# Mixture of experts on one core: gathering the tokens of eight experts at once, 40 places each, with two more weight slots

## The reference, cut to what matters

```python
g_sel = argmax(xt @ w_rg + b_rg)                 # one group per token
top_v, top_i = top_k(el_sel, 2)                  # two experts in it
gate = softmax(top_v) * p_sel                    # their weights
hid = silu(xb @ w_gate[e]) * (xb @ w_up[e])      # for the tokens xb of expert e
y[token] += (hid @ w_down[e]) * gate
ys = (silu(xt @ ws_gate) * (xt @ ws_up)) @ ws_down
y = y + sigmoid(xt @ w_sg) * ys
```

## Time and profile before

| | before |
|---|---|
| median of 3 runs | 2825.86 us (2825.48 to 2827.86) |
| profiled execution, its own time | 2827.91 us |
| its span, first to last instruction | 2826.1 us |
| mean granted TensorE clock | 0.976 |
| PE busy | 2671.8 us (95%) |
| DVE, ACT, POOL busy | 1230.1, 1096.6, 83.3 us |
| HBM read | 697.21 MB, 247 GB/s over the span |

### The profile page before, as it was taken

The page is one execution under the profiler, slowest core; times in us unless marked ns, Lnnn a source line. Parts: engine busy times, 40 slices in busy tenths (PEclk is TensorE's granted clock), DMA queues, the critical chain, the costliest instruction groups (busy, mean ns, idle before and its releaser), DMA issues.

```text
span 2826.1 us, 48229 instructions
## 1 busy us (share of the span) xinstructions
PE 2671.8 (95%) x20460; PEld 2084.1 (74%) x20460; DVE 1230.1 (44%) x2087; ACT 1096.6 (39%) x1999; POOL 83.3 (3%) x100
## 2 busy tenths in 40 slices
PE   8999888999998999999899999999898999999998
PEld 6879756887887887788787666666698776666665
DVE  5547257655556744655562112122476432112112
ACT  5445244545445623644542222222463532222222
POOL 0000000000000011000010000000002100000000
PEclk9999889999999999999999999999999999999999
DMA  8534574644544421454354999999641149999996
GB/s 341 188 123 166 211 308 197 247 185 160 213 179 164 150 77 62 158 215 179 120 200 189 411 413 417 416 412 417 264 152 61 46 169 394 415 417 413 416 417 247
DMA packets 96419, 701.53 MB, mean 248 GB/s; under 512 B 10688, under 2 KB 10816, under 8 KB 11328
## 3 DMA queue, kind: packets, MB, share of 16 engines
q1 hardware_dynamic: 96192, 698.30, 62.3%
HBM read 697.21 MB, written 1.05 MB: 247 GB/s over the span
## 4 chain that ended last, share of the span: by engine, by line
PE 88%; DVE 5%; ACT 3%; issue 2%; DMA 1%; POOL 0%; SPq 0%; DVEq 0%; ACTq 0%
PE bank L1597 16%; PE bank L834 12%; PE bank L836 12%; PE bank L835 12%; PE bank L1657 8%; PE bank L1575 5%; PE bank L1684 4%; PE bank L1930 3%; DMA weight_ring<-weight_slots 1%; PE bank L2050 1%; PE bank L1466 1%; PE bank L1469 1%; PE bank L1481 1%; PE bank L1090 1%; PE bank L561 1%
## 5 line engine op out<-in xcount | busy, mean ns | idle before, releaser
L1597 PE MATMUL bank<-weight_ring,packed_h 128*64 128x256 f32 x2176 | 285.4, 379 | 0.0
L834 PE MATMUL bank<-source_hi_lo,weight_hi_lo 128*128 128x256 f32 x864 | 250.9, 290 | 13.3 <-DVE source_hi_lo L824 8.9
L1597 PE MATMUL bank<-more_slots,packed_h 128*64 128x256 f32 x1920 | 257.0, 379 | 1.5 <-ACT packed_h L1584 1.5
L834 PE MATMUL bank<-gate_up_hi_lo,x_hi_lo 128*128 128x512 f32 x640 | 253.1, 396 | 0.5 <-DVE gate_up_hi_lo L952 0.5
L1597 PEld LDWEIGHTS bank<-weight_ring,packed_h 128*64 128x64 f32 x2176 | 196.3, 137 | 74.3 <-issue 18.1
L836 PE MATMUL bank<-gate_up_hi_lo,x_hi_lo 128*128 128x512 f32 x640 | 249.7, 390 | 0.0
L835 PE MATMUL bank<-gate_up_hi_lo,x_hi_lo 128*128 128x512 f32 x640 | 249.3, 389 | 0.0
L835 PE MATMUL bank<-source_hi_lo,weight_hi_lo 128*128 128x256 f32 x864 | 245.7, 284 | 0.0
L836 PE MATMUL bank<-source_hi_lo,weight_hi_lo 128*128 128x256 f32 x864 | 245.5, 284 | 0.0
L1597 PEld LDWEIGHTS bank<-more_slots,packed_h 128*64 128x64 f32 x1920 | 173.9, 137 | 69.8 <-issue 15.4
L793 DVE TENSOR_TENSOR weight_hi_lo<-weight_ring,weight_hi_lo 128x1024 fp32r<-128x1024 f32 x141 | 171.7, 1222 | 89.2 <-ACT weight_hi_lo L787 89.0
(11 more groups left out here) (590 smaller groups left out, 4982.1 us busy)
## 6 DMA issues: line engine op xcount, KB each, us to landing
weight_ring<-weight_slots SPq DMA_DIRECT2D x443, 1024.0 KB, 7.6
more_slots<-weight_slots SPq DMA_DIRECT2D x212, 1024.0 KB, 9.1
h_sb<-weight_slots SPq DMA_DIRECT2D x3, 1024.0 KB, 7.0
y_sb<-weight_slots SPq DMA_DIRECT2D x3, 1024.0 KB, 9.5
params_sb<-small_params SPq DMA_DIRECT2D x1, 2908.5 KB, 17.2
x_sb<-x_by_tokens SPq DMA_DIRECT2D x1, 1024.0 KB, 5.2
out_by_tokens<-x_sb SPq DMA_DIRECT2D x4, 256.0 KB, 2.5
params_sb<-small_params SPq DMA_DIRECT2D x1, 70.5 KB, 5.0
```

What stands on the lines that cost most here:

```text
L834: e.matmul(out, w[0], x[0], start=start, stop=False, skip_group_check=shared)
L1597: mm = e.matmul(ps[x * CAP:(x + 1) * CAP, m * FB:(m + 1) * FB], self.hc[:, c, (2 * (p % 2) + x) * CAP:(2 * (p % 2) + x + 1) * CAP], wt[:, ...
```

## The change

Places per expert go from 64 to 40, while the tiles of the expert products stay 64 wide (`TILE`). `select_dve` makes the matrix for eight experts at once, 320 columns, in every fourth pair; the gated copy stays a matter of four experts (`select_gates_dve`), in tiles of 64 of which 40 are written. `gather_pe` takes one chunk to a bank, four matmuls of 320 columns, eight times for eight experts; `gather_act` copies 320 columns at a time. Gathers stand in the pairs p = 3, 7, ... 27, four banks ahead of the scatter and four behind the transposes. The products of an expert read 64 columns of `hc` from its first place on, of which 24 are the next expert's. POOL clears the columns behind the last expert and the unused places of the gated copies at the start of the stage. The flag goes up above 40 tokens. The stage has seven slots of its own instead of five, `late_gates` and its transpose become parts of `packed_silu`, the unused constant goes, and the scratch size falls from 8192 to 1024.

```diff
...
 SLOT = 2048
 RING = 6
 FFN_EXTRA = 2
-MOE_EXTRA = 5
-CAP = 64
+MOE_EXTRA = 7
+CAP = 40
+TILE = 64
 FB = 256
 FFN_BLOCKS = 2816 // FB
 N_EXP = 64
...
-    pk.add("before", (s < t).astype(np.float32))
...
         self.picked, self.gates = sb("picked", [P, TT, N_EXP]), sb("gates", [P, TT, N_EXP])
         self.rank, self.most = sb("ranks", [P, TT, N_EXP]), sb("most_tokens", [P, 1])
         self.h_tok = sb("h_tokens_hi_lo", [P, 2, TT, D], F32R)
-        self.sel = [sb(f"places{j}", [P, TT, 4, CAP], F32R) for j in range(2)]
-        self.selg = [sb(f"gated_places{j}", [P, TT, 4, CAP]) for j in range(2)]
-        self.hc = sb("packed_h", [P, C, 4 * CAP])
-        self.late, self.gates_T = sb("late_gates", [P, N_EXP]), sb("late_gates_T", [N_EXP, T])
+        self.sel = [sb(f"places{j}", [P, TT, 8, CAP], F32R) for j in range(2)]
+        self.selg = [sb(f"gated_places{j}", [P, TT, 4, TILE]) for j in range(2)]
+        self.hc = sb("packed_h", [P, C, 7 * CAP + TILE])
         self.flag = k.flags[:, self.i:self.i + 1]
         inner = ExitStack()
...
         self.gate_sum, self.slot_gate = sb("gates_by_place", [P, T]), sb("place_gates", [P, 2])
         self.psilu = [sb(f"packed_silu{j}", [P, FB]) for j in range(2)]
         self.phid = [sb(f"packed_hidden{j}", [P, FB]) for j in range(2)]
+        self.late, self.gates_T = self.psilu[1][:, 0:N_EXP], self.psilu[0][0:N_EXP, :]
         self.shared_slots, waiting = [], []
...
         return buf[(p // 2) % 2][:, q, 2 * (p % 2):2 * (p % 2) + 2, :]
     def select_dve(self, e, g):
         k, n, b = self.k, self.n, g % 2
         if g == 0:
             e.wait_ge(*k.ge("ranks", n, TT - 1))
+        if g >= 2:
+            e.wait_ge(*k.ge("gathered", n, g - 2, C - 1))
+        for q in range(TT):
+            r = self.rank[:, q, 8 * g:8 * g + 8].unsqueeze(2).to_broadcast([P, 8, CAP])
+            e.tensor_tensor(self.sel[b][:, q, :, :], k.par("places").unsqueeze(1).to_broadcast([P, 8, CAP]), r, ALU.is_equal).then_inc(*k.up("places", n, g, q))
+    def select_gates_dve(self, e, h):
+        k, n, b, four_of = self.k, self.n, h % 2, slice(4 * (h % 2), 4 * (h % 2) + 4)
+        if h == 0:
             e.wait_ge(*k.ge("gates", n, TT - 1))
-        if g >= 2:
-            e.wait_ge(*k.ge("gathered", n, g - 2, 3))
-            e.wait_ge(*k.ge("turned_back", n, 2 * (g - 2) + 1))
+            e.wait_ge(*k.ge("empty_places", n, 2))
+        if h >= 2:
+            e.wait_ge(*k.ge("turned_back", n, 2 * (h - 2) + 1))
         for q in range(TT):
-            r = self.rank[:, q, 4 * g:4 * g + 4].unsqueeze(2).to_broadcast([P, 4, CAP])
-            e.tensor_tensor(self.sel[b][:, q, :, :], k.par("places").unsqueeze(1).to_broadcast([P, 4, CAP]), r, ALU.is_equal).then_inc(*k.up("places", n, g, q))
-            e.wait_ge(*k.ge("places", n, g, q))
-            e.tensor_tensor(self.selg[b][:, q, :, :], self.sel[b][:, q, :, :].bitcast(F32),
-                            self.gates[:, q, 4 * g:4 * g + 4].unsqueeze(2).to_broadcast([P, 4, CAP]), ALU.mult).then_inc(*k.up("gated_places", n, g, q))
-    def gather_pe(self, e, g, m):
-        k, n = self.k, self.n
-        ps = k.banks.take(e, (n, "gather", g, m), ("packed_h", n, g, m))
-        if m == 0:
+            e.wait_ge(*k.ge("places", n, h // 2, q))
+            e.tensor_tensor(self.selg[b][:, q, :, 0:CAP], self.sel[h // 2 % 2][:, q, four_of, :].bitcast(F32),
+                            self.gates[:, q, 4 * h:4 * h + 4].unsqueeze(2).to_broadcast([P, 4, CAP]), ALU.mult).then_inc(*k.up("gated_places", n, h, q))
+    def gather_pe(self, e, g, c):
+        k, n = self.k, self.n
+        ps = k.banks.take(e, (n, "gather", g, c), ("packed_h", n, g, c))
+        if c == 0:
             e.wait_ge(*k.ge("places", n, g, TT - 1))
-        if g == 0 and m == 0:
+        if g == 0 and c == 0:
             e.wait_ge(*k.ge("h_tok_lo", n, TT - 1, 1))
-        for j in range(2):
-            c = 2 * m + j
-            for x, (q, part) in enumerate((q, part) for q in range(TT) for part in range(2)):
-                mm = e.matmul(ps[:, j * T:(j + 1) * T], self.h_tok[:, part, q, c * P:(c + 1) * P],
-                              self.sel[g % 2][:, q, :, :].rearrange("p e s -> p (e s)"), start=x == 0, stop=x == 3)
-        mm.then_inc(*k.up("gathered", n, g, m))
-    def gather_act(self, e, g, m):
-        k, n = self.k, self.n
-        if g and m == 0:
-            e.wait_ge(*k.ge("packed_up", n, 2 * g - 1))
-        e.wait_ge(*k.ge("gathered", n, g, m))
-        e.activation(self.hc[:, 2 * m:2 * m + 2, :], halves(k.banks.at(n, "gather", g, m)), ACT.Copy).then_inc(*k.up("packed_h", n, g, m))
+        for x, (q, part) in enumerate((q, part) for q in range(TT) for part in range(2)):
+            mm = e.matmul(ps[:, 0:8 * CAP], self.h_tok[:, part, q, c * P:(c + 1) * P],
+                          self.sel[g % 2][:, q, :, :].rearrange("p e s -> p (e s)"), start=x == 0, stop=x == 3)
+        mm.then_inc(*k.up("gathered", n, g, c))
+    def gather_act(self, e, g, c):
+        k, n = self.k, self.n
+        if g and c == 0:
+            e.wait_ge(*k.ge("packed_up", n, 4 * g - 1))
+        e.wait_ge(*k.ge("gathered", n, g, c))
+        e.activation(self.hc[:, c, 0:8 * CAP], k.banks.at(n, "gather", g, c)[:, 0:8 * CAP], ACT.Copy).then_inc(*k.up("packed_h", n, g, c))
     def packed_gate_up_pe(self, e, p):
         k, n, w = self.k, self.n, self.expert_slots[p]
         ps = k.banks.take(e, (n, "packed", p), ("packed_hidden", n, p))
-        if p % 2 == 0:
-            e.wait_ge(*k.ge("packed_h", n, p // 2, 3))
+        if p % 4 == 0:
+            e.wait_ge(*k.ge("packed_h", n, p // 4, C - 1))
+        if p == 0:
+            e.wait_ge(*k.ge("empty_places", n, 0))
         for m in range(2):
             for c in range(C):
                 for x in range(2):
                     i, wt = w[2 * m + x]
                     if c == 0:
                         e.wait_ge(*k.weights.landed(i))
-                    mm = e.matmul(ps[x * CAP:(x + 1) * CAP, m * FB:(m + 1) * FB], self.hc[:, c, (2 * (p % 2) + x) * CAP:(2 * (p % 2) + x + 1) * CAP],
+                    first = (2 * (p % 4) + x) * CAP
+                    mm = e.matmul(ps[x * TILE:(x + 1) * TILE, m * FB:(m + 1) * FB], self.hc[:, c, first:first + TILE],
                                   wt[:, c * FB:(c + 1) * FB], start=c == 0, stop=c == C - 1)
             mm.then_inc(*k.up("packed_gate" if m == 0 else "packed_up", n, p))
...
                 i, wd = self.expert_slots[p][4 + x]
                 if fc == 0 and m == 0:
                     e.wait_ge(*k.weights.landed(i))
-                mm = e.matmul(ps[x * CAP:(x + 1) * CAP, :], self.turned[p % 2][:, fc * P + x * CAP:fc * P + (x + 1) * CAP],
+                mm = e.matmul(ps[x * TILE:(x + 1) * TILE, :], self.turned[p % 2][:, fc * P + x * TILE:fc * P + (x + 1) * TILE],
                               wd[:, fc * D + m * 512:fc * D + (m + 1) * 512], start=fc == 0, stop=fc == 1)
         mm.then_inc(*k.up("packed_down", n, p, m))
...
     def gathers_in(self, p):
-        g = p // 2 + 1
-        return (g, (0, 1), (2, 3)) if p % 2 and g < self.PAIRS // 2 else (g, (), ())
+        g = p // 4 + 1
+        return (g, (0, 1, 2, 3), (4, 5, 6, 7)) if p % 4 == 3 and g < self.PAIRS // 4 else (g, (), ())
     def experts_pe(self, e):
         for p in range(self.PAIRS):
...
         return over
     def experts_act(self, e):
-        for m in range(4):
-            self.gather_act(e, 0, m)
+        for c in range(C):
+            self.gather_act(e, 0, c)
         for p in range(self.PAIRS):
             if p == self.PAIRS - 1:
                 over = self.overflow_load(e)
...
             if p == self.PAIRS - 1:
                 over = self.overflow_load(e)
             self.packed_hidden_dve(e, p)
+            if p % 4 == 0 and p // 4 + 1 < self.PAIRS // 4:
+                self.select_dve(e, p // 4 + 1)
             if p % 2 == 0 and p // 2 + 1 < self.PAIRS // 2:
-                self.select_dve(e, p // 2 + 1)
+                self.select_gates_dve(e, p // 2 + 1)
             self.scatter_dve(e, p)
             self.packed_out_dve(e, p, 0)
             self.packed_out_dve(e, p, 1)
...
         self.shared_pe(e, 3)
         self.spread_pe(e, self.k.gain[:, self.i, 3, :])
         for m in range(4):
-            self.gather_pe(e, 0, m)
+            self.gather_pe(e, 0, 2 * m)
+            self.gather_pe(e, 0, 2 * m + 1)
             if m < 3:
                 self.shared_down_pe(e, m + 1)
         over = self.experts_pe(e)
...
             self.shared_dve(e, u)
         self.ranks_dve(e)
         self.select_dve(e, 0)
+        self.select_gates_dve(e, 0)
         self.shared_dve(e, 3)
         over = self.experts_dve(e)
         self.overflow_dve(e, over)
         self.back_dve(e, lambda f: k.ge("gain_row", self.n, f))
     def pool(self, e):
+        k, n = self.k, self.n
+        for signal in self.begun():
+            e.wait_ge(*k.ge(*signal))
```

(4 more changed lines are left out.)

## The result

| | before, same chip | changed |
|---|---|---|
| median of 4 runs | 2826.86 us (2825.48 to 2828.77) | 2795.90 us (2791.26 to 2799.56) |
| ratio | | 0.9893 (0.988 to 0.9905) |
| profiled execution | 2827.91 us | 2793.84 us, span 2792.0, mean granted clock 0.976 |
| params load | 2908.5 KB | 2832.5 KB |

The change makes the kernel 31 us faster, where 39.0 were forecast. The same file among the experiments gave 2792.26 us and 35 us. The first measurement lies 9 us above the forecast, outside the range that was given to the forecast's own mechanism (2782 to 2792) and at the upper edge of the wide one (2778 to 2796). The second lies 5 us above the forecast, at the edge of the narrow range.

A forecast was written before the change was run, and what follows sets the result against it. PE was taken to bound the mixtures, with weights close behind. Per stage -25.8 + 5.8 + 0.8 - 0.2 = -19.4 us; two stages -38.8, constant -0.2: -39.0, so 2786.9 us, range 2778 to 2796 (own 2782 to 2792).

The forecast's parts named there:

- the forecast's own mechanism: Whole kernel: PE stays the bound and the summed terms hold, 2786.9 us, own range 2782 to 2792; chance 0.70.
- Fewer and wider gathers: Mixture pairs: 7 gather pairs instead of 15, 25.8 us less a stage; 320 columns at 152 ns, 5.8 us more.
- the cheap nor the dear price of 320 columns: Gather rivals: 320 columns cost as 256, 2774 to 2783 us, chance 0.12; or as 512, 2828 us, chance 0.03.
- second pass: Flag rival: it goes up above 40 tokens and 192 slots load again, 3260 us or more; chance 0.01.
- Two more slots: Mixture weights: 2.47 us a slot, last lands 2 to 8 us early; slots cover the gathers' gain, alone give nothing.
- the weights become the bound: Mixture rival: 2.53 us a slot, last lands 2.3 us late, a stage gains 17.1 us, 2791.5 us; chance 0.10.
- DMA was idle behind the stage: Behind the mixture: DMA share 0.02, so the next stage finds its six slots; no cost in the sum.
- The heads: Head of each mixture: 0.8 us more for 32 wider gather matmuls, 0.2 less for ACT's last copy.
- the 0.2 for the constants: Kernel start: 64 KB of constants fewer to load ahead of awaited weights, 0.2 us less.
- The bank: Gather pairs: fourth and eighth gathers find their banks free, no wait, 0.25 us to spare; 0.05 short at 126 ns.
- no change: Summary of chances: result within 0.2%, some 5.6 us, of the kernel before; given 0.04.
- slower: Summary of chances: kernel slower than before by more than 0.2%; given 0.02.

The follow-up runs named there:

- before_seven: The kernel before with seven own slots instead of five and scratch size 1024 instead of 8192, nothing else: 2827.24 us, ratio 1.0012.
- places32: The changed kernel with 32 places per expert instead of 40, gathers of 256 columns, tokens beyond 32 left out, flag held down: 2783.95 us, ratio 0.9849.

## Why the forecast was right, and where it failed

**Fewer and wider gathers: right.** Gather pairs of 17.66 us, others of 13.56, 153 ns a matmul, 7 such pairs, the granted clock at 1.00: 458.5 us a mixture whenever PE is the bound; 459 was forecast, and 458.5 is what its terms for the experts give. Neither the cheap nor the dear price of 320 columns came true, and no second pass ran.

**"Two more slots": failed on size, and looked at the wrong slot.** The step took 2.47 us a slot from four microseconds in the head, or 2.50 from one pair, and let the last slot land 2 to 8 us early. The landing times give 2.51 us as a mean with a full queue: 2.49 from slot to slot, and about five breaks of some 1 us in a mixture that a short window doesn't hold. The last slot landed 458.24 us after the first gate product in the first mixture, and 457.47 in the second, against 451.9 to 457.1 in the working.

That alone would still have been early: PE, left to itself, starts the last down products at 458.5. The step held only this last slot against PE, and said that earlier ones have more room. The up slots of the same pair have less: they are wanted 6.5 us before the down products and land only 5 us before the last slot. In the first mixture the second up slot landed at 453.28 us, and PE, which could have had it at about 452.0, went on at 453.32 (the row at 1994.10 above). In the second it landed at 451.37, in time. The first mixture lost 1.5 us, the second 0.1.

The rival "the weights become the bound" had the right mechanism, but 2.53 us a slot and 2.3 us a stage: it is closer in the first mixture, the forecast's zero in the second. That the slots cover what the gathers gain and give nothing by themselves was right, and measured: 9 to 10 us with the gathers, none without.

The Trainium skill ("DMA: Bandwidth & Descriptors", "Where 436 GB/s comes from") lets about 358 GB/s from HBM bind a load; the mixtures sustained 418 to 427 on one active core, so the trace disagrees here too. The same section's 435 GB/s for the fabric is not passed by any rate here: 1 MiB in 2.435 us is 430.6 GB/s, the fastest seen in a run of slots.

**"DMA was idle behind the stage", so the next stage's loads cost nothing: failed.** The loads do arrive in time for Delta. What they do is lengthen the jumps of ACT and DVE over the second pass, which are on the path in the tail: 1.9 us, a term that the sum had at nothing. The idle DMA was the state of before, in which these loads had already landed; the two slots alone are enough to move them (`before_seven`, 16.9 us). The forecast asked when the data would be there, not what ran beside the transfer. The pause ahead of the table load (1.90 us) was in the trace of before all along.

**The heads: right within what can be told.** The second cost 0.6 us more, as forecast; the first 1.6. About 0.9 of it is one step, the router's logits, which took 4.56 us instead of 3.63 at a granted clock of 0.78 instead of 1.00 in this execution. The heads of one kernel differ by 1 us between executions: the three profiles of the kernel before have 58.8, 59.9 and 59.9 in the first and 60.6, 59.8 and 59.8 in the second, the two of the changed kernel 60.5, 59.5 and 61.3, 60.5.

**The rest.** Forecast 39.0, shown for the profiled pair 34.1: 1.5 lost in the first mixture, 1.9 in the tail, 1.0 in the first head, and a few tenths, among them the 0.2 for the constants, which no row shows. The medians of the two measurements give 31 and 35. What is left between them and the profiled sum is of the size of what Delta's clock does; the forecast took the clock as it was in the one profile of before. Whether the earlier end of the mixture makes the low clock more likely there, or whether these profiles happened to fall so, is open: one profile is taken of each kernel, and no experiment moved the clock by itself.

**The bank: right, with less to spare.** No wait shows at 153 ns a matmul; 0.15 us does at 116 ns. At 126 ns, in `places32`, PE goes on 0.14 us behind the end of `scatter`, and the pair takes 17.04 us where the same 32 matmuls of 256 columns, in four banks, made it 16.80. So being short cost 0.24 us there and not the 0.05 worked out, and with those 0.14 us the quarter of a microsecond to spare is about 0.1.

**The chances.** Two entries of the summary are off by 0.01: "no change" is 0.03 + 0.02 = 0.05, "slower" 0.01.

## What to carry to other kernels

When a change takes time from one engine and the next bound is a few microseconds away, cost that bound with the mean over hundreds of transfers, not with the best short window: 2.47 against 2.51 us a slot was nearly the whole reserve. Hold every transfer of the last round against the time at which it is wanted, not only the last one. Look at what runs beside a transfer that moves, even if its data is early. And matmuls under 256 columns here cost nearly as much as those of 256: the way to cheaper gathers was fewer, not narrower.

## What the runs showed of the hardware

- The rate of a load depended on its place in SBUF: 2.435 us for 1 MiB at one place within 256 bytes, 2.484 to 2.490 at two others. The cause wasn't looked into. It is worth nothing while PE is the bound, and 12 us (2790.0 to 2777.7) where it isn't.
- A jump of ACT over a long stretch of code held it for 1.90 us with DMA at 0.02 and 2.87 us with DMA at 0.51; DVE came 1.9 us later. Without the jumps, beside the same loads, ACT didn't stand still there.
- Distances of matmuls with a weight load of 128 columns ahead of each: 116 ns at 160 columns, 126 at 256, 153 at 320, 231 at 512.
- A stage of small matmuls takes 234 to 244 us by how much of it PE is granted 1.2 instead of 2.4 GHz (mean granted clock 0.965 to 0.905), with no change in its code.
